# Narrower moving operands in the triangular inversions of a two-block hybrid layer

## The chip, the cores and the metric

The kernel is one program on one core of a Trainium2 chip. The metric is the device time of an execution in microseconds. Three executions of the kernel before are known, and one more was recorded by the hardware profiler. All times below are from these.

## What is computed

The reference runs two different transformer-like blocks, one after the other, on 256 tokens of width 2048, in float32. Only the two places that need the inverse of a triangular matrix matter here.

The first block holds a gated delta rule with 8 heads and chunks of 64 tokens:

```
lmat = where(strict, k_beta @ k.T * decay, 0)              # 64 x 64 per chunk and head
sol  = triangular_solve(eye + lmat, rhs, lower=True, unit_diagonal=True)
```

The second block holds a recurrence over tokens, forward and backward, with 16 heads of 64:

```
sa = S @ nkk_t
S  = S * w_t + sa b_t^T + v_t k_t^T
```

The kernel computes it in chunks of 64 tokens too, and each chunk needs the inverse of a unit triangular 64x64 matrix.

## The kernel before

Nearly all of the span is projections: weights come from memory in pieces, are split on ScalarE and VectorE into a high and a low part, and TensorE multiplies both by the activations (lines 267 to 290). The delta rule (about 570 to 790 us) is interwoven with the projection of a gated unit (`glu`, lines 608 to 610). The recurrence (about 2190 to 2720 us) runs alone: no projection lies beside it.

An inverse is built by doubling. Let T be the inverse of the block diagonal with blocks of size w. Level l (w = 2^l, l = 1 to 5) makes it into the one with blocks of 2w by two products with a mask between them:

1. the mask product, A times T, into one PSUM bank (`b[0]`);
2. VectorE multiplies it by the level's mask and keeps the w columns out of every 2w that the mask leaves, packed, in `i_p` (line 1151). At level 5 in the "tt" form it masks all 64 columns (line 1149);
3. the sum product, T times that, into a second place in PSUM (`b[1]`);
4. VectorE adds the result to the columns of T concerned (lines 1163 and 1160), and below level 5 transposes T into its second copy (line 1167).

So only 32 of a 64-column row are used by a level. `lower(ap, b)` is the strided view of them (runs of b out of 2b), `packed(ap, b)` the view of the first 32 columns as runs of b, `narrow(bank)` the four 64-column blocks of a bank.

In the **recurrence** one inversion works on 2 directions by 4 blocks by 2 halves of the partitions: 16 matmuls of 64x64 by 64 columns for each product (`blocks_pe`, line 1117). The two halves are products on opposite corners of the array, `half(0)` to `half(0)` and `half(1)` to `half(1)`. There are 16 inversions (8 pairs of heads, context and sequence), hence 160 products. The turns of `phases` (line 2005) weave the inversion (`V`) with the chunk steps (`C`), the preparation of the next unit (`P`) and the finishing of the last (`O`) on each engine, in the order of `PERIOD` (line 1565).

In the **delta rule** one inversion works on 4 blocks by 2 halves: 8 matmuls for each product (`halves_pe`, line 1063), 4 inversions, 40 products.

All these operands are float32, and the trace shows each float32 matmul as two records of TensorE, each with its own weight load (PEld): 5,120 records on line 1117 and 640 on line 1063.

In the kernel before every one of these matmuls moves 64 columns. The mask product moves all of T. The sum product moves the 32 packed columns of `i_p` twice, through a broadcast view. The last sum product of the "tt" form moves all 64 columns of `i_tt`.

Of the kernel before, what the change touches and what calls it, by code (L numbers as in the profile page):

```python
# [16 lines left out]
ALU = mybir.AluOpType  # L17
# [13 lines left out]
C = 64  # L31
# [62 lines left out]
def program(nc, d):  # L94

    ctx = ExitStack()
    with ctx:
        base = (nc.sbuf_base + 63) // 64 * 64

        def sb(name, shape, offset, dt=F32):  # L100
            return nc.alloc_sbuf_tensor_at(name, [P] + list(shape), dt, offset=base + int(offset * KB))
# [79 lines left out]
        i_a = sb("i_a", [4, C], TMP)  # L181
        i_t = sb("i_t", [4, C], TMP + 2)
        i_tt = sb("i_tt", [4, C], TMP + 4)
        i_p = sb("i_p", [4, C], TMP + 6)
# [245 lines left out]
        def settle(eng):  # L430


            eng.sem_inc(settled, 1)
# [619 lines left out]

        def halves_pe(pe, by_pe, out, lhs, rhs):

            for m in range(4):
                for r in (slice(0, C), slice(C, P)):
                    o, w = out[r, m * C:m * C + C], rhs[r, m, :]  # L1060
                    if w.shape[1] < C:
                        o, w = o.rearrange("p (a s) -> p a s", a=2), w.unsqueeze(1).broadcast_to([C, 2, C // 2])
                    mm = pe.matmul(o, lhs[r, m, :], w, start=True, stop=True)
            mm.then_inc(by_pe, 1)

        def invert_pe(pe, n, one):
            by_pe, by_dve, (i_a, i_t, i_tt, i_p), b, want = one
            for l in range(1, 6):
                pe.wait_ge(by_dve, n * 17 + (3 if l == 1 else 3 * l - 1))
                halves_pe(pe, by_pe, b[0], i_a, i_t)  # L1070
                yield
                pe.wait_ge(by_dve, n * 17 + 3 * l + 1)
                if l < 5:
                    halves_pe(pe, by_pe, b[1], i_tt, i_p[:, :, 0:C // 2])
                else:
                    halves_pe(pe, by_pe, b[1], i_p, i_tt)
                yield

        def invert_dve(dve, n, sets):
            inv_first_dve(dve, n, sets, d_mask)  # L1080
            yield
            for l in range(1, 6):
                inv_mask_dve(dve, n, sets, l, d_mask)
                yield
                inv_sum_dve(dve, n, sets, l)
                yield
# [3 lines left out]
        def lower(ap, b, first=0):  # L1090

            return ap.rearrange("p m (k s) -> p m k s", s=2 * b)[:, :, :, first:first + b]

        def packed(ap, b):

            return ap[:, :, 0:C // 2].rearrange("p m (k s) -> p m k s", s=b)

        def narrow(bank, first=0):
            return bank[:, first:first + 4 * C].rearrange("p (m s) -> p m s", m=4)

        def all4(mask):
            return k_masks[:, mask:mask + 1, :].broadcast_to([P, 4, C])

        def blocks_pe(pe, n, sets, k, outs, lhs, rhs):

            for swap in range(2):
                if not swap:
                    settle(pe)
                mm = [None, None]
                for m in range(4):  # L1110
                    for e in range(2):
                        r = half(e ^ swap)
                        w = rhs[e][r, m, :]
                        o = outs[e][r, m * C:m * C + C]
                        if w.shape[1] < C:
                            o, w = o.rearrange("p (a s) -> p a s", a=2), w.unsqueeze(1).broadcast_to([C, 2, C // 2])
                        mm[e] = pe.matmul(o, lhs[e][r, m, :], w, start=True, stop=True)  # L1117
            for e in range(2):
                mm[e].then_inc(sets[e][0], 1)

        def inv_mask_pe(pe, n, sets, l):
            for by_pe, by_dve, (i_a, i_t, i_tt, i_p), b, want in sets:
                pe.wait_ge(by_dve, n * 17 + (3 * l if l == 1 else 3 * l - 1))
            blocks_pe(pe, n, sets, 2 * l - 1, [s[3][0] for s in sets], [s[2][0] for s in sets], [s[2][1] for s in sets])

        def inv_sum_pe(pe, n, sets, l):
            for by_pe, by_dve, (i_a, i_t, i_tt, i_p), b, want in sets:
                pe.wait_ge(by_dve, n * 17 + (3 * l + 1))
            lhs = [i_p if l == 5 and want == "tt" else i_tt for _, _, (i_a, i_t, i_tt, i_p), b, want in sets]
            rhs = [i_tt if l == 5 and want == "tt" else i_p[:, :, 0:C // 2] for _, _, (i_a, i_t, i_tt, i_p), b, want in sets]  # L1130
            blocks_pe(pe, n, sets, 2 * l, [s[3][1] for s in sets], lhs, rhs)

        def inv_first_dve(dve, n, sets, all4):
# [9 lines left out]
        def inv_mask_dve(dve, n, sets, l, all4):  # L1143
            w = 2 ** l
            for by_pe, by_dve, (i_a, i_t, i_tt, i_p), b, want in sets:
                dve.wait_ge(by_pe, n * 10 + (2 * l - 1))
                m = all4(l)
                if l == 5 and want == "tt":
                    dve.tensor_tensor(i_p, narrow(b[0]), m, ALU.mult).then_inc(by_dve, 1)
                else:  # L1150
                    dve.tensor_tensor(packed(i_p, w), lower(narrow(b[0]), w), lower(m, w), ALU.mult)\  # L1151
                       .then_inc(by_dve, 1)

        def inv_sum_dve(dve, n, sets, l):
            w = 2 ** l
            for by_pe, by_dve, (i_a, i_t, i_tt, i_p), b, want in sets:
                dve.wait_ge(by_pe, n * 10 + 2 * l)
                if l == 5 and want == "tt":
                    out = lower(i_tt, w, w)
                    dve.tensor_tensor(out, lower(narrow(b[1]), w, w), out, ALU.add).then_inc(by_dve, 1)  # L1160
                else:
                    out = lower(i_t, w)
                    dve.tensor_tensor(out, packed(narrow(b[1]), w), out, ALU.add).then_inc(by_dve, 1)
            if l < 5:
                for by_pe, by_dve, (i_a, i_t, i_tt, i_p), b, want in sets:
                    dve.wait_ge(by_dve, n * 17 + (3 * l + 2))
                    dve.transpose(i_tt, i_t).then_inc(by_dve, 1)
# [127 lines left out]
        def dn_pe(pe, i):  # L1295
# [41 lines left out]
            pe.wait_ge(*dnv.at(i, "init"))  # L1337
            pe.wait_ge(*dna.at(i, "bv"))
            yield from invert_pe(pe, i, inv[0])
            pe.wait_ge(inv[0][1], i * 17 + 17)  # L1340
            for c in range(NCH):
# [632 lines left out]
        def half(a):  # L1974
            return slice(64 * a, 64 * a + 64)
# [306 lines left out]
        def inverse_pe(pe, j, x):  # L2282
            yield
            pe.wait_ge(j_done[1][1], inv_no(j, x) * 17 + 3)
            settle(pe)
            for l in range(1, 6):
                inv_mask_pe(pe, inv_no(j, x), jinv[x], l)
                yield
                inv_sum_pe(pe, inv_no(j, x), jinv[x], l)
                yield  # L2290
# [4 lines left out]
        def inverse_dve(dve, j, x):  # L2295
            dve.wait_ge(*pre_v[x].at(j, "im1"))
            inv_first_dve(dve, inv_no(j, x), jinv[x], all4)
            yield
            for l in range(1, 6):
                inv_mask_dve(dve, inv_no(j, x), jinv[x], l, all4)  # L2300
                yield
                inv_sum_dve(dve, inv_no(j, x), jinv[x], l)
                yield
# [1027 lines left out]
```

## Time and profile before

| What | Value |
|---|---|
| time of three executions, median (lowest to highest) | 3584.18 us (3581.43 to 3584.95) |
| the profiled execution's own time | 3591.9 us |
| its span, first to last instruction | 3590.1 us |
| mean granted clock of TensorE | 0.97 of full speed |
| PE busy, share of the span | 3381.0 us (94%), 28442 records |
| PEld (weight loads) | 2915.5 us (81%), 28442 records |
| DVE | 2470.7 us (69%) |
| ACT | 1588.0 us (44%) |

PE is TensorE's matmuls, PEld its weight loads, DVE is VectorE, ACT ScalarE. The busy time of PE counts every matmul from its start to its modelled end, and matmuls are pipelined, so 94% is not 94% of what the array can do: the pitch, the time from one start to the next, tells more than the length. A granted clock of 1.00 in a stretch is 2.4 GHz, 0.50 is 1.2 GHz.

### The profile page before, as it was taken

To read this page: it belongs to the slowest core of one execution; us is meant where nothing else is said; L and a number is where in the kernel's file an instruction comes from. 1 tells how busy PE (TensorE), PEld (TensorE's weight loads), DVE (VectorE), ACT (ScalarE), POOL (GpSimd) and SP (SyncE) were. 2 spreads that over 40 slices of the span, in tenths; PEclk is the share of its full clock that TensorE was granted. 3 is DMA by queue.
4 is the path that set the end of the run, shared out by engine and by line. 5 is a ranking of instruction groups with operands and counts; after the bars stand their busy time and mean duration, and the time that the engine had idled before them with its cause. 6 is when DMAs were issued, how large, how long until landed. Compare 5 with 4: busy or idle time off the path is not lost. (4 is left out here: it accounts for less than half of the span.)

```text
span 3590.1 us, 73988 instructions
## 1 busy us (share of the span) xinstructions
PE 3381.0 (94%) x28442; PEld 2915.5 (81%) x28442; DVE 2470.7 (69%) x4291; ACT 1588.0 (44%) x2475; POOL 248.0 (7%) x415
## 2 busy tenths in 40 slices
PE   9999998999899999999899987888888899999998
PEld 8998887788788888888788965766667788888887
DVE  5769995656777778777765864667665766666555
ACT  5547773334444444444212344444443444444433
POOL 0000000000000000111111202111110000000000
PEclk9999998999999999999999997999998999999999
DMA  5446662235455555776444720000003466665553
GB/s 196 180 154 241 247 251 82 83 118 189 162 184 184 183 186 186 260 244 246 157 170 172 275 69 12 7 7 7 8 6 129 165 225 226 225 224 202 190 188 134
DMA packets 94341, 572.25 MB, mean 159 GB/s; under 512 B 12657, under 2 KB 14961, under 8 KB 37521
## 3 DMA queue, kind: packets, MB, share of 16 engines
q1 hardware_dynamic: 72000, 493.49, 37.8%
q0 software_dynamic: 22096, 75.32, 6.1%
q8 instruction: 177, 2.90, 0.3%
q14 instruction: 68, 0.55, 0.0%
HBM read 566.66 MB, written 2.10 MB: 158 GB/s over the span
## 5 line engine op out<-in xcount | busy, mean ns | idle before, releaser
L246 ACT ACTIVATE w_hi<-raw 128x1024 fp32r<-128x1024 f32 (+1 forms) x877 | 908.8, 1041 | 948.9 <-PE po L290 638.4
L253 DVE TENSOR_TENSOR w_lo<-raw,w_hi 128x1024 fp32r<-128x1024 f32 x880 | 1044.5, 1199 | 176.5 <-ACT w_hi L246 166.1
L289 PE MATMUL po<-hh,w_hi 128*128 128x512 f32 x2816 | 991.1, 398 | 16.9 <-DVE hh L398 8.8
L290 PE MATMUL po<-hh,w_lo 128*128 128x256 f32 x2816 | 787.4, 280 | 0.0
L289 PEld LDWEIGHTS po<-hh,w_hi 128*128 128x128 f32 x2816 | 530.5, 188 | 146.8 <-issue 18.1
L290 PEld LDWEIGHTS po<-hh,w_lo 128*128 128x128 f32 x2816 | 532.3, 189 | 0.0
L289 PE MATMUL po<-ff,w_hi 128*128 128x512 f32 x1408 | 494.3, 397 | 3.2 <-DVE w_lo L253 3.2
L290 PE MATMUL po<-ff,w_lo 128*128 128x256 f32 x1408 | 393.0, 279 | 0.0
L289 PEld LDWEIGHTS po<-ff,w_hi 128*128 128x128 f32 x1408 | 264.9, 188 | 67.1 <-DVE w_lo L253 3.9
L267 PE MATMUL po<-hh,w_lo 128*128 128x256 f32 x928 | 266.3, 287 | 0.6 <-DVE w_lo L253 0.5
L290 PEld LDWEIGHTS po<-ff,w_lo 128*128 128x128 f32 x1408 | 265.8, 189 | 0.0
L268 PE MATMUL po<-hh,w_hi 128*128 128x256 f32 x928 | 262.5, 283 | 0.0
L269 PE MATMUL po<-hh,w_hi 128*128 128x256 f32 x928 | 262.5, 283 | 0.0
L1623 PE MATMUL po<-hh,w_hi 128*128 128x512 f32 x704 | 217.8, 391 | 0.0
L554 POOL DMA_DIRECT2D late_w<-ada_late x256 | 137.8, 539 | 1138.5 <-DVE late_sum L567 835.6
L492 DVE TENSOR_REDUCE f_sum<-po 128x512 f32 (+1 forms) x132 | 91.3, 692 | 141.8 <-PE po L290 141.8
L567 DVE SCALAR_TENSOR_TENSOR late_sum<-late_w,cve,late_sum 128x512 f32<-128x512 f32 x240 | 179.2, 747 | 9.0 <-DMA late_w<-ada_late 5.8
L267 PEld LDWEIGHTS po<-hh,w_lo 128*128 128x128 f32 x928 | 177.9, 192 | 6.0 <-issue 5.0
L268 PEld LDWEIGHTS po<-hh,w_hi 128*128 128x128 f32 x928 | 177.9, 192 | 0.2
L269 PEld LDWEIGHTS po<-hh,w_hi 128*128 128x128 f32 x928 | 177.9, 192 | 0.0
L608 PE MATMUL po<-hh,w_lo 128*128 128x256 f32 x512 | 155.1, 303 | 1.0 <-DVE pa L3042 1.0
L1623 PEld LDWEIGHTS po<-hh,w_hi 128*128 128x128 f32 x704 | 132.9, 189 | 27.7
(581 smaller groups left out, 6251.2 us busy)
## 6 DMA issues: line engine op xcount, KB each, us to landing
raw<-ffn_up SPq DMA_DIRECT2D x176, 1024.0 KB, 4.8
raw<-w_in SPq DMA_DIRECT2D x112, 1024.0 KB, 4.9
late_w<-ada_late POOLq DMA_DIRECT2D x256, 256.0 KB, 4.2
raw<-ffn_down SPq DMA_DIRECT2D x64, 1024.0 KB, 5.1
raw<-ada SPq DMA_DIRECT2D x32, 1024.0 KB, 7.0
raw<-w_out SPq DMA_DIRECT2D x32, 1024.0 KB, 4.8
raw<-ffn_down SPq DMA_DIRECT2D x32, 768.0 KB, 4.2
raw<-glu SPq DMA_DIRECT2D x16, 1024.0 KB, 4.8
```

The lines of the kernel that those rows point to most:

```text
L246: act.activation(w_hi[:, k % 4, 0:width], raw[:, k // 2 % ring, (k % 2) * PW:(k % 2) * PW + width], ACT.Copy).then_inc(hi_ready, 1)
L253: dve.tensor_tensor(w_lo[:, k % 4, 0:width], raw[:, k // 2 % ring, (k % 2) * PW:(k % 2) * PW + width], w_hi[:, k % 4, 0:width].bitcast(F32 ...
L267: pe.matmul(po[bank][:, 0:T], lo, act_hi[:, t, :], start=first and n == 0, stop=False)
L268: pe.matmul(po[bank][:, 0:T], hi, act_lo[:, t, :], start=False, stop=False)
L269: mm = pe.matmul(po[bank][:, 0:T], hi, act_hi[:, t, :], start=False, stop=end)
L289: pe.matmul(halves(bank), hi, pair[:, :, t, :], start=first and n == 0, stop=False)
L290: mm = pe.matmul(po[bank][:, 0:T], lo, pair[:, 0, t, :], start=False, stop=last and n == len(tiles) - 1)
L492: return dve.tensor_reduce(out, po[bank][:].rearrange("p (s t) -> p t s", s=2), AX.X, ALU.add)
L554: pool.dma_start(late_w[:, n % 4], d["ada_late"][n:n + 1].rearrange("a p w -> p (a w)")).then_inc(late_landed[n % 4], 16)
L567: dve.scalar_tensor_tensor(out, w, col, out, ALU.mult, ALU.add).then_inc(late_step, 1)
L608: pe.matmul(bank(i * per + o), lo, act_hi[:, t, :], start=first, stop=False)
L1623: mm = pe.matmul(po[o % 4][:].rearrange("p (s t) -> p s t", s=2), w, hh[:, :, part, t, :], start=half == 0 and n == 0 and w is lo, stop=ha ...
```

## The change

Every matmul of an inversion gets the 32 columns that its level uses, and no more. A new helper `moved` takes the moving operand as it is (3 dimensions: its width decides) or as a strided view (4 dimensions, runs of s), and gives the output 32 contiguous columns. The mask product below level 5 now moves `lower(i_t, 2 ** l)`; the "t" form does so at level 5 too. The sum product moves `i_p`'s 32 columns once. The last sum product of the "tt" form moves the upper 32 columns of `i_tt`. Only the mask product of level 5 in the "tt" form still moves 64 (128 of the recurrence's 2,560 matmuls, 32 of the delta rule's 320). VectorE reads the result from packed columns of PSUM where it read it strided, with the same number of elements.

```
+        def moved(out, r, m, rhs):
+            w = rhs[r, m]
+            if len(rhs.shape) == 3:
+                return out[r, m * C:m * C + rhs.shape[2]], w
+            k, s = rhs.shape[2:]
+            return out[r, m * C:m * C + k * s].rearrange("p (k s) -> p k s", s=s), w
...
         def halves_pe(pe, by_pe, out, lhs, rhs):
...
-                    o, w = out[r, m * C:m * C + C], rhs[r, m, :]
-                    if w.shape[1] < C:
-                        o, w = o.rearrange("p (a s) -> p a s", a=2), w.unsqueeze(1).broadcast_to([C, 2, C // 2])
+                    o, w = moved(out, r, m, rhs)
...
-                halves_pe(pe, by_pe, b[0], i_a, i_t)
+                halves_pe(pe, by_pe, b[0], i_a, lower(i_t, 2 ** l) if l < 5 else i_t)
...
-                    halves_pe(pe, by_pe, b[1], i_p, i_tt)
+                    halves_pe(pe, by_pe, b[1], i_p, i_tt[:, :, C // 2:C])
...
         def blocks_pe(pe, n, sets, k, outs, lhs, rhs):
...
-                        w = rhs[e][r, m, :]
-                        o = outs[e][r, m * C:m * C + C]
-                        if w.shape[1] < C:
-                            o, w = o.rearrange("p (a s) -> p a s", a=2), w.unsqueeze(1).broadcast_to([C, 2, C // 2])
+                        o, w = moved(outs[e], r, m, rhs[e])
...
         def inv_mask_pe(pe, n, sets, l):
...
+            rhs = [i_t if l == 5 and want == "tt" else lower(i_t, 2 ** l) for _, _, (i_a, i_t, i_tt, i_p), b, want in sets]
...
         def inv_mask_dve(dve, n, sets, l, all4):
...
-                    dve.tensor_tensor(packed(i_p, w), lower(narrow(b[0]), w), lower(m, w), ALU.mult)\
+                    dve.tensor_tensor(packed(i_p, w), packed(narrow(b[0]), w), lower(m, w), ALU.mult)\
...
         def inv_sum_dve(dve, n, sets, l):
...
-                    dve.tensor_tensor(out, lower(narrow(b[1]), w, w), out, ALU.add).then_inc(by_dve, 1)
+                    dve.tensor_tensor(out, packed(narrow(b[1]), w), out, ALU.add).then_inc(by_dve, 1)
```

No engine's instructions change their number or their order: on PE the inversion's matmuls stand where they stood, 32 columns wide in place of 64, and the queues of DVE, ACT, POOL and SP read the same.

## Rows read from the trace of the kernel before

**Rows 1.** The page's chain of work that ended last, shares of the span by line.

```profile
PE po L289 15%; PE po L290 8%; PE pa L1117 2%; PE po L1117 1%; DVE k_S L2407 0%; DVE k_ln L2463 0%; DVE k_ah L2235 0%; DVE j_p L1151 0%; PE pa L2335 0%; PE po L2352 0%; PE pa L2113 0%; PE pa L2352 0%; PE po L2087 0%; PE pa L2132 0%; PE pa L2049 0%
```

**Rows 2.** The recurrence: the chain's shares by line, then busy time in 50 us stretches.

```profile
by line: issue 14.3%; PE pa L1117 11.2%; PE po L1117 9.0%; DVE k_S L2407 2.6%; DVE k_ah L2235 2.2%; DVE j_p L1151 2.1%; PE pa L2113 2.0%; DVE k_ln L2463 2.0%; PE po L2087 1.9%; PE pa L2132 1.9%; PE pa L2049 1.8%; DVE k_nt L2261 1.7%; PE pa 
core 0: us, PE busy (x) PEld busy (x) DVE busy (x) ACT busy (x) POOL busy (x), PEclk, DMA share, GB/s
...
sum 500.00, PE 421.17 PEld 347.58 DVE 338.15 ACT 223.36 POOL 88.43; mean PE 42.12 PEld 34.76 DVE 33.82 ACT 22.34 POOL 8.84
```

**Rows 3.** Line 1117: its records, and who waited for it (us, times).

```profile
L1117 PEld LDWEIGHTS po<-j_p,j_work x1280: 129/135/227, 2204.7 to 2697.1; 64*64 64x64 f32 x183
L1117 PE MATMUL po<-j_p,j_work x1280: 218/218/366, 2204.7 to 2697.2; 64*64 64x64 f32 x183
...
  DVE j_p L1151: 58.7, 34
  DVE j_work L1163: 35.3, 37
  DVE j_p L1149: 6.4, 15
  DVE j_inv_c L1160: 4.5, 8
  DVE j_inv_l L1160: 4.4, 8
```

**Rows 4.** Line 1063: who waited for it (us, times).

```profile
  DVE i_t L1163: 19.4, 16
  DVE i_p L1151: 10.8, 10
```

**Rows 5.** Timeline of TensorE, one recurrence product from 2409 us (start us, length us).

```profile
2409.09 0.22 PE L1117 MATMUL pa<-j_inv_c,j_p 64*64 64x64 f32 x1
...
2409.85 0.22 PE L1117 MATMUL pa<-j_inv_c,j_p 64*64 64x64 f32 x1
```

**Rows 6.** Timeline of TensorE, line 2087: products on four quarters of the array.

```profile
2440.15 0.24 PE L2087 MATMUL pa<-k_ah,k_kh 64*64 64x64 f32 x1
...
2440.39 0.22 PE L2087 MATMUL po<-k_ah,k_kh 64*64 64x64 f32 x1
```

**Rows 7.** Timeline: 128-column weights with 2 (line 532) and 64 (line 1797) moving columns.

```profile
328.89 1.05 PE L532 MATMUL po<-ada_sel,ada_row 128*128 128x2 f32 x8
...
328.89 0.97 PEld L532 LDWEIGHTS po<-ada_sel,ada_row 128*128 128x128 f32 x8 [0.86 <-issue]
...
2111.81 2.54 PEld L1797 LDWEIGHTS po<-t_v,t_pt 128*128 128x128 f32 x22
```

**Rows 8.** Lines 532 (128 columns of weights) and 1680 (32, 256 moving): min/median/max ns.

```profile
L532 PEld LDWEIGHTS po<-ada_sel,ada_row x64: 186/192/192, 328.9 to 556.8; 128*128 128x128 f32 x64
...
L1680 PEld LDWEIGHTS pa<-n_sqs,n_sel x32: 106/110/110, 2005.1 to 2057.0; 128*32 128x32 f32 x32
L1680 PE MATMUL pa<-n_sqs,n_sel x32: 379/379/404, 2005.1 to 2057.3; 128*32 128x256 f32 x32
```

**Rows 9.** VectorE's steps of the inversion (min/median/max ns).

```profile
L1151 DVE TENSOR_TENSOR j_p<-pa,k_masks x64: 273/291/293, 2204.1 to 2692.0; 128x128 f32<-128x128 f32 x64
...
L1163 DVE TENSOR_TENSOR j_work<-pa,j_work x64: 279/292/293, 2206.7 to 2693.8; 128x128 f32<-128x128 f32 x64
```

**Rows 10.** Busy time and granted clock (PEclk) in chosen stretches, columns as in rows 2.

```profile
2253.80:2264.00 10.20, 9.63 (x134) 7.76 (x132) 4.47 (x13) 6.05 (x12) 1.41 (x2) 0.50 0.05 15
...
2315.00:2325.00 10.00, 7.86 (x171) 6.37 (x171) 5.45 (x18) 6.15 (x14) 1.02 (x2) 1.00 0.06 16
...
2414.30:2427.90 13.60, 12.53 (x108) 8.55 (x108) 3.97 (x15) 5.47 (x12) 1.41 (x2) 0.50 0.05 12
...
2690.00:2697.50 7.50, 5.90 (x170) 5.42 (x172) 5.31 (x19) 1.24 (x4) 0.00 (x0) 1.00 0.01 3
2697.50:2711.00 13.50, 12.05 (x125) 9.10 (x119) 4.11 (x14) 3.79 (x12) 0.00 (x0) 0.63 0.00 1
```

More of the change, by code:

```diff
@@ L1123, in inv_mask_pe @@
                 pe.wait_ge(by_dve, n * 17 + (3 * l if l == 1 else 3 * l - 1))
-            blocks_pe(pe, n, sets, 2 * l - 1, [s[3][0] for s in sets], [s[2][0] for s in sets], [s[2][1] for s in sets])
+            rhs = [i_t if l == 5 and want == "tt" else lower(i_t, 2 ** l) for _, _, (i_a, i_t, i_tt, i_p), b, want in sets]
+            blocks_pe(pe, n, sets, 2 * l - 1, [s[3][0] for s in sets], [s[2][0] for s in sets], rhs)
         def inv_sum_pe(pe, n, sets, l):
@@ L1129, in inv_sum_pe @@
             lhs = [i_p if l == 5 and want == "tt" else i_tt for _, _, (i_a, i_t, i_tt, i_p), b, want in sets]
-            rhs = [i_tt if l == 5 and want == "tt" else i_p[:, :, 0:C // 2] for _, _, (i_a, i_t, i_tt, i_p), b, want in sets]
+            rhs = [i_tt[:, :, C // 2:C] if l == 5 and want == "tt" else i_p[:, :, 0:C // 2] for _, _, (i_a, i_t, i_tt, i_p), b, want in sets]
             blocks_pe(pe, n, sets, 2 * l, [s[3][1] for s in sets], lhs, rhs)
```

## The prediction

> **What bounds the kernel now.** I read the page's chain first. The longest lines in it are projections, 289 and 290; line 1117, the recurrence's inversion, holds about 3% of the span [rows 1]. So the question belongs to one stage. In the recurrence, the chain by line and the table of stretches stand side by side: line 1117 holds 11.2% and 9.0% of 500 us, about 101 us, the largest share of any line, while VectorE is busy 338 of the 500 [rows 2]. No engine is full. The stage is a chain of handovers: a product on TensorE, a mask or a sum on VectorE, the next product. What counts there is how long a product takes from its first matmul to the end of its last. In the delta rule the products stand between those of the gated unit, which fill TensorE.
>
> **What a product costs, and what sets it.** One recurrence product is two streams, one per corner of the array, each of 16 records. The timeline of one stream has starts at 2409.09 and at 2409.85 with 13 steps between them: 0.76 / 13 = 58.5 ns a step [rows 5]. A step has two things in it that overlap: moving 64 columns and loading 64 columns of weights for the next.
> - *Moving.* 64 columns last 218 ns [rows 3], 256 last 379 [rows 8]: (379 - 218) / 192 = 0.84 ns a column, so 64 columns stream for 54 ns and 32 for 27.
> - *Loading.* 64 columns last 135 ns [rows 3], 32 last 110 [rows 8]: 0.8 ns a column, 51 ns for 64.
> - *Issue.* It isn't the limit: line 2087, whose products lie on four quarters of the array in place of two corners, starts 16 records from 2440.15 to 2440.39, 16 ns apart [rows 6], where line 1117 starts one every 29 ns.
>
> So moving and loading are nearly equal now, and the step of 58.5 ns is either's time with some 5 ns on top. The change halves the first and leaves the second. What a step does when only the load is long is read where weights of 128 columns meet few moving ones: the loads of 8 matmuls with **2** columns take 0.97 us from the first start to the last end, (0.97 - 0.19) / 7 = 111 ns a step, where 0.19 is the length of one such load [rows 8]; those of 22 matmuls with **64** columns take 2.54 us, (2.54 - 0.19) / 21 = 112 ns a step [rows 7]. Thirty-two times the columns, the same step: there the load sets it. Half such a load would be 56 ns.
>
> [...]
>
> **The change, part by part.**
> - *The steps of a product.* Bounds: unchanged at 58.5 ns, or 56, the half of 111. I take 58.5, the nearest row, which is this very load in this very place. The other end is 15 steps of 2.5 ns, 0.04 us a product; on the products that VectorE waited for (next point) 87 x 0.04 = 3.3 us.
> - *The end of a product.* The last matmul ends 27 ns sooner. This is worth something where VectorE stood waiting. In the recurrence it waited 34 + 37 + 8 + 8 = 87 times at lines 1151, 1163 and 1160 [rows 3]: 87 x 27 = 2.3 us. The 15 waits of line 1149 follow the product that keeps 64 columns. In the delta rule it waited 16 + 10 = 26 times [rows 4]: 0.7 us at most, since the gated unit's products stand behind. Together -3 us. Where VectorE was late anyway, its own queue (chunk steps, preparation) hides the gain.
> - *VectorE.* It reads packed columns of PSUM where it read strided ones. Line 1151 (strided) and line 1163 (packed) have the same size and take 291 and 292 ns [rows 9]: nothing, with no cover needed.
> - *The strided view.* At level 1 the moving operand is runs of 2 elements. No row shows such a read. It can't beat contiguous columns, so no gain; up to 54 ns for 32 columns it lies under the load and costs nothing beyond the 27 ns at the end. I take nothing. If runs of 2 took twice the old 54 ns, the 16 mask products of level 1 would grow by 15 steps of 50 ns each: +12 us.
> - *The clock.* I take no change; the other end is in the second rival.
>
> The sum is -3 us on the profiled execution of 3591.9 us (its span 3590.1). That execution stands 7.7 us above the median of 3584.18, and the difference carries over: **3581 us**. The terms' ends give 3577 to 3585. A measurement here can tell about 0.2%, 7.2 us, so my forecast is no change.
>
> **Rival 1, faster: the step falls.** If the 58.5 ns are moving time and a load of 64 rows and columns is cheaper than half of a full one, the step goes to 27 + 5 = 32 ns, 45% less. On 101 us of chain that is 46 us, and some 4 in the delta rule (40 products x 7 steps x 27 ns is 7.5, half of it hidden): 3534 us. VectorE's own work would be next to end late and may keep half: 3559. For it: none of these rows has 64-column weights with fewer than 64 moving columns. Against it: rows 7, and the load's 51 ns, which don't care what is moved. It decides if a step falls below 55 ns.
>
> **Rival 2, slower: TensorE is granted its low clock for longer.** The recurrence already runs partly at 1.2 GHz: 2253.8 to 2264 and 2414.3 to 2427.9 at 0.50 [rows 10], and three more such stretches of the recurrence, not shown, end as these two do while inversion products run. At the end of the recurrence the inversion's products held 1.00 (170 records in 7.5 us); then the chunk steps ran alone (125 in 13.5 us) and the clock fell to a mean of 0.63 [rows 10]. So these products are what keeps the clock up in the thin places, and the change takes half their columns away. At the low clock VectorE, as the measure of progress, is busy 8.4 of 23.8 us, at the full one 5.5 of 10 in a thin part of a turn [rows 10]: 10 us at the low clock cost 1 - 0.35 / 0.55, some 3.6 us; against its mean of 338 of 500 [rows 2], 4.8. Say 4.2. If each of the five stretches ends 5 us later (11 us) and two new ones of 10 us come (8 us), it is +19 - 3: 3600 us; half of the 19 gives 3591. I put its centre at 3596. Against it: thin stretches with 171 records in 10 us hold 1.00 [rows 10], the number of records stays, and so does the time of the loads; if those count as work, nothing changes. It decides once the low stretch that begins near 2414 us lasts clearly over 13.6 us.
>
> [...]
>
> **Rival 3, slower: the strided read** as priced above, 3593 us. That the change doesn't narrow the matmuls is no rival: the order of the changed program has them at 32 columns.
>
> **How the numbers follow.** Forecast 0.44, rival 1 0.15, rival 2 0.38, rival 3 0.03. Of the forecast 0.37 lies within 0.2% and 0.07 below, should the step also shrink to 56 ns. Rival 1 is faster throughout. Rival 2 in its milder forms (0.07) stays within, else it is slower (0.31). Faster 0.22, same 0.44, slower 0.34. Cases of both signs weigh much, so the forecast's own range, 3577 to 3585, stands beside the whole one, 3563 to 3606: it leaves out rival 1 nearly entire and the far end of rival 2, somewhat under 2 in 10.
>
> **What the changed profile would show.** Right: records of line 1117 about 191 ns long in place of 218, with starts in a stream still 56 to 59 ns apart; VectorE's waits on them shorter by about 0.03 us each; the recurrence within 5 us of its length; granted clocks as before. Wrong: steps near 32 ns (rival 1), or a recurrence longer by 10 us and more with more of it at 0.50 (rival 2), or steps of level 1's mask products longer than those of the other levels (rival 3).

## The result and the profile after

The changed kernel takes **3725.82 us** (median of 5 runs, 3720.63 to 3754.32), the kernel before, run beside it, 3584.95 us (5 runs, 3581.43 to 3599.81). The ratio is 1.0394, 95% interval 1.0368 to 1.0421: slower by about 141 us. The forecast was 3581 us, the range 3563 to 3606, and slower had a chance of 0.34.

The page of the changed kernel first: the busy times, TensorE's busy tenths and granted clock in 40 slices of the span, and the chain by engine and by line.

```profile
PE 3579.4 (95%) x28442; PEld 3093.9 (82%) x28442; DVE 2469.0 (66%) x4291; ACT 1589.7 (42%) x2475; POOL 243.7 (6%) x415
...
PE   9999998999899999998999879989998899999998
...
PEclk9999997989999999999999976565566999999999
...
PE 38%; DVE 2%; issue 1%; ACT 0%; DVEq 0%; POOL 0%; ACTq 0%
PE po L289 15%; PE po L290 7%; PE pa L1120 4%; PE po L1120 3%; PE pa L2326 1%; PE pa L2091 1%; PE po L2091 1%; PE pa L2352 1%; PE pa L2339 0%; PE pa L2053 0%; PE pa L2073 0%; PE po L2356 0%; PE pa L2356 0%; PE pa L2117 0%; PE po L2073 0%
```

And the line of the granted clock on the page of the kernel before:

```profile
PEclk9999998999999999999999997999998999999999
```

The number of matmuls is the same (28,442 before and after), nearly half of the inversion's columns are gone, and yet TensorE is busy 198 us longer, and VectorE as long as before (2469.0 against 2470.7 us). The inversion of the recurrence, line 1117 before, is line 1120 here. Its share of the page's chain went from 3% [rows 1] to 7%. The difference that meets the eye is the clock: eight slices in a row of 5 to 7 tenths where the kernel before has 9 almost throughout. They are the recurrence. The mean granted clock of the span went from 0.970 to 0.901. With the two levels 1.00 and 0.50 that is (1 - 0.970) / 0.5 x 3590.1 = 215 us at 1.2 GHz before and (1 - 0.901) / 0.5 x 3752.5 = 743 us after, 528 us more. (The profiled execution of the changed kernel is the slowest of the five; the other four had 0.906 to 0.908, which is 685 to 700 us.)

Two stretches of 50 us in the middle of the recurrence, by engine (busy us, records, then the granted clock, DMA share and GB/s), in the kernel before:

```profile
2300.00:2350.00 50.00, 43.09 (x1079) 36.59 (x1080) 36.80 (x112) 21.56 (x54) 10.15 (x14) 1.00 0.02 6
2350.00:2400.00 50.00, 41.03 (x952) 34.00 (x948) 36.54 (x112) 28.29 (x66) 11.76 (x16) 1.00 0.03 8
```

and in the changed kernel:

```profile
2300.00:2350.00 50.00, 47.88 (x722) 39.37 (x720) 24.96 (x81) 17.02 (x39) 7.32 (x11) 0.57 0.02 5
2350.00:2400.00 50.00, 47.86 (x848) 42.09 (x846) 29.76 (x91) 15.61 (x38) 5.61 (x8) 0.60 0.02 6
```

Read them across. By its records TensorE is *busier* after (47.88 us of 50 against 43.09), and so are its weight loads (39.37 against 36.59); but it gets through 722 records in place of 1079, and VectorE, whose work per turn has not changed, through 81 instructions in place of 112. The clock is 0.57 where it was 1.00. The longer busy time is in part its effect: records last longer at the low clock, as the lines of line 1120 below show. Timed from the last turn of the attention to the last matmul with `k_bd` (line 2423 before, 2427 after) the recurrence takes 683.7 us, before 553.0: 131 us of the 162 by which the two spans differ. Most of the rest lies in the delta rule. The whole recurrence as one stretch, before and after:

```profile
2171.60:2724.60 553.00, 455.83 (x9843) 371.80 (x9842) 349.23 (x1072) 239.69 (x571) 96.11 (x131) 0.90 0.03 8
```

```profile
2196.30:2880.00 683.70, 623.30 (x9843) 521.49 (x9842) 348.02 (x1072) 241.09 (x571) 92.05 (x131) 0.59 0.02 6
```

The work is the same, 9843 records of TensorE and 1072 instructions of VectorE. By the clocks, (1 - 0.90) / 0.5 x 553.0 = 111 us of it ran at the low level before and (1 - 0.59) / 0.5 x 683.7 = 561 us after. TensorE, idle for 97 us of this stage before, is idle for 60 us now.

The step itself did what the forecast said at the full clock. One stream of a product at the full clock in the changed kernel, by the timeline (start us, length us), to be held against [rows 5]:

```profile
2369.62 0.21 PE L1120 MATMUL pa<-j_work,j_a_c 64*64 64x32 f32 x1 [0.82 <-DVE j_inv_c L1145]
2369.67 0.22 PE L1120 MATMUL pa<-j_work,j_a_c 64*64 64x32 f32 x1
...
2370.52 0.22 PE L1120 MATMUL pa<-j_work,j_a_c 64*64 64x32 f32 x1
```

15 steps in 0.90 us, 60 ns, with 32 columns; [rows 5] had 58.5 ns with 64. Another product, where the low clock is granted:

```profile
2288.00 0.31 PE L1120 MATMUL pa<-j_work,j_a_c 64*64 64x32 f32 x1
2288.12 0.29 PE L1120 MATMUL pa<-j_work,j_a_c 64*64 64x32 f32 x1
...
2289.62 0.29 PE L1120 MATMUL pa<-j_work,j_a_c 64*64 64x32 f32 x1
```

15 steps in 1.62 us, 108 ns. Over all neighbouring records of a stream the median step is 58 ns at the full clock and 107 ns at the low one, in both kernels. What changed is how many fall on each: counted from the starts in the trace, 338 of line 1117's 4,800 steps run at the low clock before (7%); after, 3,540 of the 4,560 steps with 32 columns (78%).

Records of line 1120 (min/median/max ns) and VectorE's waits on it (us, times), against those in [rows 3]:

```profile
L1120 PEld LDWEIGHTS po<-j_p,j_work x1280: 129/223/228, 2229.5 to 2851.4; 64*64 64x64 f32 x183
L1120 PE MATMUL po<-j_p,j_work x1280: 192/291/313, 2229.5 to 2851.5; 64*64 64x32 f32 x183
...
L1120 PE MATMUL pa<-j_inv_c,j_p x128: 219/219/313, 2253.5 to 2817.4; 64*64 64x32 f32 x128
...
  DVE j_p L1155: 99.5, 54
  DVE j_work L1167: 68.2, 62
```

The first two lines are mostly of the low clock, with medians of 223 ns for a load and 291 ns for a matmul; the third, of level 5, is mostly of the full clock, at 219 ns. VectorE waits 54 times for 1.84 us each where it waited 34 times for 1.73 us, and 62 times for 1.10 us where it waited 37 times for 0.95 us: more often, and longer.

### The profile page after: what moved, and what is told of

Its sections match the earlier page's. It is cut to its first block and busy times, and to the rows that moved or that the text cites. A ratio compares the mean times of both kernels' runs of the same rounds, so it can differ in the third digit from the quotient of the medians.

```text
span 3752.5 us, 73988 instructions
## 1 busy us (share of the span) xinstructions
PE 3579.4 (95%) x28442; PEld 3093.9 (82%) x28442; DVE 2469.0 (66%) x4291; ACT 1589.7 (42%) x2475; POOL 243.7 (6%) x415
```

## Experiments

The theory after the result: the change lowers the number of columns that TensorE moves in the thin places of the recurrence, the low clock is granted for longer, and everything on TensorE there runs slower. The rivals: the strided read, VectorE's packed reads of PSUM, or the narrow matmul as such. All runs are put beside runs of the kernel before on the same chip; their median is 3586.75 us for the first four kernels, 3585.85 us for the half dose, the other columns and the first two fills, and 3592.96 us for the last three runs (twice the columns, the last two fills). The time at the low clock is worked out from span and mean clock, as above.

### Moving the 32 columns twice

The changed kernel with everything that it reads and packs, but each 32-column view goes through the array twice, as in the kernel before:

```diff
-                return out[r, m * C:m * C + rhs.shape[2]], w
+                return o.rearrange("p (a s) -> p a s", a=2), w.unsqueeze(1).broadcast_to([C, 2, C // 2])
             k, s = rhs.shape[2:]
-            return out[r, m * C:m * C + k * s].rearrange("p (k s) -> p k s", s=s), w
+            return o.rearrange("p (a k s) -> p a k s", a=2, s=s), w.unsqueeze(1).broadcast_to([C, 2, k, s])
```

> The changed kernel, but every 32-column view is moved twice into neighbouring columns of PSUM (through a broadcast), so that each matmul streams 64 columns again; the strided view, the packed reads of VectorE and the order stay. Theory (the clock is granted less because the inversion's matmuls stream half the columns): back to the kernel before, 3575 to 3605 us, low clock (0.50) for about 200 to 260 us of the span in place of 744. Rival A (the strided view or the packed reads are what costs): stays near 3726 us, 3700 or more.

Measured: 3589.78 us (10 runs) against 3586.75, ratio 1.0009 (0.9989 to 1.0029). The loss is gone. The stretch of the recurrence that stood at 0.57 above, in this kernel:

```profile
2300.00:2350.00 50.00, 43.48 (x958) 35.56 (x954) 33.80 (x104) 26.04 (x60) 11.05 (x16) 0.97 0.03 8
```

The span's mean clock is 0.971, some 208 us at the low level, as before the change. The strided view and VectorE's packed reads are both still in it, so neither is the cause. What is left is the number of columns that a matmul moves and writes; moving and writing were not told apart.

### The same columns without a stride

The mask product moves the first 32 columns, which lie side by side, in place of those of the level, so that it computes another matrix.

```diff
-                halves_pe(pe, by_pe, b[0], i_a, lower(i_t, 2 ** l) if l < 5 else i_t)
+                halves_pe(pe, by_pe, b[0], i_a, i_t[:, :, 0:C // 2] if l < 5 else i_t)
...
-            rhs = [i_t if l == 5 and want == "tt" else lower(i_t, 2 ** l) for _, _, (i_a, i_t, i_tt, i_p), b, want in sets]
+            rhs = [i_t if l == 5 and want == "tt" else i_t[:, :, 0:C // 2] for _, _, (i_a, i_t, i_tt, i_p), b, want in sets]
```

> The changed kernel, but the mask product below level 5 moves the first 32 contiguous columns of T in place of the strided 32 (so it computes another matrix). Theory (clock): as the changed kernel, 3705 to 3755 us, since 32 columns are streamed as before. Rival A (the strided read costs): most of the 141 us is gone, under 3640 us.

Measured: 3727.5 us (2 runs), ratio 1.0394 (1.0342 to 1.0445), the ratio of the change itself. The stride costs nothing that shows, from the other side too.

### Each stage alone

The change in the delta rule alone, and in the recurrence alone. In each the other stage has its former products and VectorE reads them as before.

```diff
-            rhs = [i_t if l == 5 and want == "tt" else lower(i_t, 2 ** l) for _, _, (i_a, i_t, i_tt, i_p), b, want in sets]
+            rhs = [i_t for _, _, (i_a, i_t, i_tt, i_p), b, want in sets]
...
-            rhs = [i_tt[:, :, C // 2:C] if l == 5 and want == "tt" else i_p[:, :, 0:C // 2] for _, _, (i_a, i_t, i_tt, i_p), b, want in sets]
+            rhs = [i_tt if l == 5 and want == "tt" else i_p[:, :, 0:C // 2] for _, _, (i_a, i_t, i_tt, i_p), b, want in sets]
```

(This is the delta rule alone; for the recurrence alone the same is done in `invert_pe`.)

> Only the delta rule's inversion moves 32 columns; the recurrence moves 64 as before. Theory (clock): the delta rule's stage ends later by what its low-clock stretches add (its low clock grew from about 34 to 103 us between 556 and 782 us of the profiled executions, the stage's end moved by some 22 us): 3595 to 3615 us. Rival (all of the loss lies in the recurrence, which runs alone): 3580 to 3592 us.

> Only the recurrence's inversion moves 32 columns; the delta rule moves 64 as before. Theory (clock): the larger part of the loss, 3695 to 3715 us, low clock in the recurrence (2190 to 2860 us) as in the changed kernel. Rival (the two stages share the loss evenly): near 3655 us.

Measured: the delta rule alone 3613.52 us (7 runs), ratio 1.0050 (1.0019 to 1.0081), some 280 us at the low clock. The recurrence alone 3718.1 us (4 runs), ratio 1.0362 (1.0315 to 1.0409), some 660 us. The two losses, 0.50% and 3.62%, add up to 4.1%, within the interval of the whole. The first time is within what was expected and the second 3 us above it. Each stage pays by itself. The delta rule loses too, although the gated unit's products stand beside its inversion: the cover that the prediction named there did not hide this.

### Half of the dose

Only the mask product moves 32 columns; the sum product moves its 32 twice again.

```diff
-                return out[r, m * C:m * C + rhs.shape[2]], w
+                o = out[r, m * C:m * C + C]
+                if rhs.shape[2] == C:
+                    return o, w
+                return o.rearrange("p (a s) -> p a s", a=2), w.unsqueeze(1).broadcast_to([C, 2, C // 2])
```

> The changed kernel, but the sum product of both inversions moves its 32 columns twice again, as before; only the mask product moves 32. Theory (the clock falls because fewer columns stream through TensorE): half of the products are narrow, so the loss lies between nothing and the change's 141 us, and the low-clock time of the span between 219 and 744 us; I expect 3620 to 3690 us. Rival (the narrow product itself is slow, its read or its write, whatever the clock): the loss is in proportion, 3655 us, at an unchanged granted clock of 0.97.

Measured: 3630.99 us (4 runs), ratio 1.0137 (1.0111 to 1.0162), mean clock 0.950, some 363 us at the low level. In the recurrence:

```profile
2300.00:2350.00 50.00, 43.28 (x997) 36.94 (x994) 36.59 (x114) 24.27 (x58) 11.47 (x16) 0.90 0.03 9
2350.00:2400.00 50.00, 44.57 (x828) 35.50 (x825) 29.44 (x91) 23.28 (x55) 6.51 (x10) 0.77 0.03 8
```

The time is in the expected range, and the clock is not the unchanged 0.97 of the rival. A little under half of the narrow products (1,280 of 2,720 matmuls, since the mask products of level 5 in the "tt" form were not narrowed) bring about a third of the loss (1.37%, 49 of 141 us) and 28% of the added low-clock time (148 of 528 us). The loss is nearer to the time at the low clock than to the number of narrow products; in proportion to the products the ratio would have been 1.0185, outside the interval.

### Other columns beside the narrow products

The changed kernel, and ahead of each of the recurrence's products two matmuls more whose result nobody reads. They move as many columns as the change took away; the 16 matmuls that count stay 32 wide.

```diff
                 if not swap:
                     settle(pe)
+                    for e in range(2):
+                        pe.matmul(outs[e][half(e), 4 * C:8 * C], lhs[e][half(e), 0, :], sets[e][2][1][half(e)],
+                                  start=True, stop=True)
```

> The changed kernel, and in each product of the recurrence's inversion two more matmuls ahead of it, that move 256 columns each with 64x64 weights into half of the bank that nothing reads: more work, and as many moved columns per product as before the change, although the 16 matmuls that count stay 32 wide. Theory (moved columns keep the clock up): low clock in the recurrence falls back to about that of before, and the time falls although work was added, to 3610 to 3670 us (the two matmuls take some 0.25 to 0.5 us in each of 160 products, of which a part is hidden). Rival (the narrow matmuls themselves cost, or lower the clock, whatever runs beside them): the added work comes on top, 3765 to 3800 us.

Measured: 3724.71 us (4 runs), ratio 1.0377 (1.0342 to 1.0412): neither figure. But the clock answered. The mean is 0.937, some 470 us at the low level in place of 743, and two stretches and the whole recurrence read:

```profile
2300.00:2350.00 50.00, 44.02 (x1024) 36.27 (x1020) 33.30 (x102) 19.07 (x49) 5.85 (x8) 0.99 0.02 5
2350.00:2400.00 50.00, 46.43 (x903) 37.41 (x904) 27.85 (x87) 24.64 (x56) 11.46 (x16) 0.91 0.03 8
...
2190.20:2853.90 663.70, 594.90 (x10482) 481.55 (x10482) 342.63 (x1072) 240.74 (x571) 93.00 (x131) 0.77 0.02 7
```

In the recurrence that is (1 - 0.77) / 0.5 x 663.7 = 305 us at the low level, in place of 561; it is not back at the 111 us of before, as I had expected. In the first of these stretches the narrow matmuls ran at 0.99, with other columns sent through the array ahead of them. So the rival in its second form, that the narrow matmul lowers the clock whatever runs beside it, is out.

The time stayed the same as that of the change. An estimate of why: the fill isn't cheap. Its step is 266 ns at the full clock by the starts in the trace, and each stream has two of its records in a product, so 160 x 2 x 266 ns = 85 us, and more where the clock is low; my expectation had 40 to 80 us, of which I had taken a part to be hidden. Against it stand 273 us less at the low clock. The change paid 162 us of span for its 528 us, 0.31 us for each, so they are worth 85 us. The two cancel, and 1 us less was measured; no run separates them.

### Twice the columns

The kernel before, with each matmul of the recurrence's products moving its columns twice, 128 in place of 64.

```diff
-                        w = rhs[e][r, m, :]
-                        o = outs[e][r, m * C:m * C + C]
-                        if w.shape[1] < C:
-                            o, w = o.rearrange("p (a s) -> p a s", a=2), w.unsqueeze(1).broadcast_to([C, 2, C // 2])
+                        o, w = wide(outs[e], r, m, rhs[e][r, m, :])
```

(`wide` gives a view of both halves of the bank and the moving operand through a broadcast of 2.)

> The kernel before, but each matmul of the recurrence's inversion products moves its columns twice, 128 in place of 64, the second copy into the half of the bank that nothing reads. Theory (the step is the longer of the weight load, 58 ns, and of the time to stream the columns): 128 columns hold the step at 100 to 110 ns at the full clock, 8 steps of some 49 ns more in each of 160 products are 63 us, of which TensorE pays nearly all: 3620 to 3660 us at a granted clock of 0.97 or above. Rival (the load alone holds the step even at 128 columns): no slower than before, and up to 15 us faster by a higher clock.

Measured: 3674.5 us (2 runs), ratio 1.0232 (1.0186 to 1.0277). The timeline of one stream:

```profile
2381.50 0.27 PE L1121 MATMUL pa<-j_work,j_a_l 64*64 64x128 f32 x1
2381.61 0.27 PE L1121 MATMUL pa<-j_work,j_a_l 64*64 64x128 f32 x1
2381.71 0.27 PE L1121 MATMUL pa<-j_work,j_a_l 64*64 64x128 f32 x1
```

The median step at the full clock is 109 ns, 0.85 ns a column: here the columns set it. Over the three widths, 58 ns for 32, 58 for 64 and 109 for 128, the step fits the longer of a load's time and the columns' time. The step is the theory's, and the time lies above its range (3620 to 3660 us). The size was wrong by a miscount: a stream has 16 records in a product, as the prediction says, not 8. 160 x 15 x 51 ns are 122 us, of which 83 showed. The clock in this recurrence:

```profile
2300.00:2350.00 50.00, 47.27 (x920) 41.85 (x916) 31.75 (x101) 20.50 (x50) 9.84 (x14) 1.00 0.02 6
2350.00:2400.00 50.00, 44.73 (x820) 38.18 (x817) 29.46 (x91) 22.86 (x54) 6.08 (x9) 1.00 0.03 8
```

This row beside that of the change is the shortest sign that busy time by records doesn't tell the clock: 47.27 us busy at 1.00, 47.88 us busy at 0.57 (there lengthened by the low clock itself).

### Filling the idle places of the kernel before

If columns hold the clock up, the kernel before may gain by columns where TensorE stands idle before its low stretches. `fill_pe` issues matmuls of 128x128 weights (the identity) and 256 columns into a bank's half that nobody reads.

```diff
             for e in range(2):
+                if first_unit(j, x):
+                    fill_pe(pe, 3 if e else 12)
                 pe.wait_ge(*pre_g[x].at(j, f"kh{e}"))
...
             pe.wait_ge(*ota.at(7, "q"))
+            fill_pe(pe, 8)
             pe.wait_ge(low_a, 3)
```

> The kernel before, and 23 matmuls of 128x128 weights and 256 columns in the three waits of TensorE that open the recurrence (4.9, 6.6 and 2.1 us idle between 2171 and 2191 us of the span), their result unread. Theory (a stretch of idle TensorE starts the 37.5 us of low clock at 2171.9): those 37.5 us shrink to under 15, and as TensorE is busy in about 60% of them the kernel gains 3 to 12 us, 3573 to 3582 against 3585. Rival (the low stretch comes from the small matmuls that follow, or the filler is late and holds up the work): no change or 2 to 6 us slower.

The second kernel adds, in `phases`, a fill at the end of the loop's turn:

```diff
                 tile(i * 2 + 2, 0)
+                if eng is nc.tensor:
+                    eng.wait_ge(j_done[0][1], inv_no(i * 2 + 3, "c") * 17 + 17)
+                    fill_pe(eng, 5)
```

> As the filler at the start, and 5 such matmuls more at the end of each turn of the recurrence's loop, where TensorE waits 3.4 us at 2411.6 before 13.7 us of low clock (and again near 2544). Theory: these two stretches go too, 3 to 12 us less than the filler at the start alone, 3564 to 3580. Rival: the 2.2 us of filler come late in each of three turns and hold up the chunk that follows, 3 to 7 us slower than the filler at the start alone.

Measured: at the start alone 3588.33 us, ratio 1.0004 (0.9986 to 1.0023); with the turns 3589.18 us, ratio 1.0010 (0.9993 to 1.0028), 12 runs each (one of the second kernel took 7627 us and is not in its ratio). The gains of 3 to 12 us that the theory had for each did not come. At the start the low clock did go: the 50 us that begin 11.6 us before the end of the attention had a clock of 0.62 in the kernel before, and 0.90 with the fill. The rows, of the kernel before:

```profile
2160.00:2210.00 50.00, 30.55 (x313) 24.31 (x315) 12.61 (x36) 24.79 (x56) 9.45 (x14) 0.62 0.06 20
```

and of the kernel with the fill at start and turns:

```profile
2147.10:2197.10 50.00, 38.69 (x423) 32.02 (x424) 14.41 (x42) 25.71 (x57) 11.89 (x18) 0.90 0.07 20
```

In its profile the recurrence took 541.1 us in place of 553.0, so it ran once more, with a third kernel that also fills the gaps of the last chunk:

```diff
                     mm.then_inc(Q.did(f"u{e}_{s}"), 1)
+                if x == "l" and isinstance(j, int) and j == 7:
+                    fill_pe(pe, 1)
...
                     mm.then_inc(Q.did(f"d{e}_{s}"), 1)
+                if x == "l" and isinstance(j, int) and j == 7:
+                    fill_pe(pe, 3)
```

> The kernel before with filler at the start and at the loop's turns, once more. In the profile its recurrence took 541.1 us against 553.0 before, but the runs showed no gain. Theory (the gain of the stage is real and variation of the other stages hid it): 8 to 14 us under the kernel before. Rival (the stage gains in the profiled execution alone): within 5 us of the kernel before.

> As the filler at the start and the turns, and filler also between the steps of the last chunk, where the trace of before has 34.1 us of low clock from 2701.0 with TensorE mostly idle. Theory (its small matmuls lie on the chain, and run at half speed there): low clock in the span falls from 160 to about 130 us and the recurrence gains 2 to 6 us more in the profile. Rival (the filler holds up the chain's matmuls): the recurrence is 2 to 8 us longer than without the filler in the last chunk.

Measured: once more 3586.47 us, ratio 0.9981 (0.9962 to 0.9999), the recurrence 549.7 us in this profile (and 13.7 us at 0.50 from 2407.7 us on, near the place where the kernel before has its own from 2414.3); with the last chunk 3589.23 us, ratio 0.9990 (0.9970 to 1.0010), the recurrence 552.6 us. The expectation for the last chunk failed: its profile has the same 180 us at the low level as the one without it, not 130, and its recurrence is 2.9 us longer, which its rival had. No version here is shown to beat the kernel before by more than the scatter of these runs. The gain of 8 to 14 us expected of the repeated kernel is not borne out, and a small gain of a few us is neither shown nor excluded: the two ratios of the same kernel average 0.9996. Some 36 to 51 us less at the low clock in their profiles (mean clocks 0.975 and 0.977) bought next to nothing, while the change paid 0.31 us for each such us. Those stretches lie where TensorE waits most (30.55 us busy of 50 in the row above), so a faster clock there finds little to shorten, and the fill takes its own time; which of the two weighs more was not separated.

## Why the prediction was wrong

**The step that failed is "The clock. I take no change"**, and with it the price of rival 2. The mechanism was named there: the change takes half of the columns of the products that keep the clock up, and TensorE is granted its low clock for longer. Its size was off by a factor of ten: five stretches of the recurrence 5 us longer and two new ones of 10 us, 45 us in all, against 450 us measured there (561 - 111), and the delta rule, which the rival left out, lost 0.50% alone. Its price per us, 0.42, was too high but of the right order: the recurrence grew by 131 us, 131 / 450 = 0.29.

The sign by which it was to be told held at once: "the low stretch that begins near 2414 us lasts clearly over 13.6 us". In the changed kernel the table of stretches has there, and just before (by time, not by work: its recurrence begins 25 us later):

```profile
2372.50:2416.90 44.40, 43.38 (x608) 36.03 (x604) 20.94 (x64) 11.77 (x30) 5.52 (x8) 0.50 0.01 2
...
2420.30:2444.20 23.90, 23.01 (x383) 19.95 (x382) 15.91 (x48) 9.92 (x23) 4.19 (x6) 0.50 0.01 3
```

Why was it priced so low? Two readings led there.

- *The rows of the high clock were read as a reserve.* [rows 10] shows 171 records in 10 us at 1.00, and the text set that against the rival: the number of records stays, and so does the time of the loads. But a record's time was 58 ns of load *and* 54 ns of columns then; the change leaves the first and halves the second. The runs show which of the two counts here: the changed kernel and the one that moves its columns twice have the same matmuls and the same loads, and the stretch from 2300 us had 0.57 in the one and 0.97 in the other. The busy time of the loads can't tell it, 39.37 us of 50 against 35.56 us, because a load lasts longer at the low clock.
- *Only the thin places were priced.* The rival lengthened five known low stretches. What it should have asked is what the busy middle of the recurrence, 2300 to 2400 us at 1.00, would do with half the columns. The answer is the 0.57 and 0.60 above.

The Trainium skill, "TensorE: Matmul & The Clock Gate", section "What's actually happening", has the throttled state as the default that activity releases, and the trace agrees: with fewer columns the recurrence falls back to it, with a mean of 0.59 in place of 0.90. The Trainium skill, same page, section "Why this matters for your kernels", puts a fall in the middle of a kernel down to idle gaps between bursts of matmuls. By that rule the low stretch from 2372.5 us would not have come: the longest idle time of TensorE in the 15 us ahead of it is 0.90 us, shorter than the gaps which that section names, and in the stretch itself TensorE is busy 43.38 of 44.40 us and the clock stays at 0.50. Here the measurement decides: the same matmuls and loads had the low clock with 32 columns and the high one with 64.

Point by point, the rest of the working:

- *The step stays at 58.5 ns*: right. 58 ns at the full clock with 32 columns. The Trainium skill, same page, section "Back-to-back issue gap", says that in a stream of loads and matmuls both set the spacing. The trace agrees: 58 ns for 32 and for 64 columns, as [rows 7] had it for a longer load, and 109 ns for 128, where the columns take over.
- *The last matmul ends 27 ns sooner*: wrong, and the whole of the forecast's -3 us rested on it. At the full clock a record with 32 columns lasts 219 ns (the level 5 line of line 1120 above; 1,053 of 1,086 such records last 219 ns or more) where one with 64 lasted 218 [rows 3]; 21 alone reach 192 ns. The last record of a stream with 32 columns has 219 ns each time that it ran at the full clock. At the low clock it is 291 ns against 311, but lost there in the longer steps. VectorE's waits grew in place of shrinking.
- *VectorE's packed reads and the strided view cost nothing*: right. Line 1155, which was 1151 [rows 9], has 274/292/293 ns, and the two runs that kept or removed the stride differ from their partners by less than their intervals.
- *Rival 1, the step falls to 32 ns*: out, by the same 58 ns.
- *Where the 131 us of the recurrence come from*: the chain by line over the recurrence, before and after (the lines are cut off at their end in the view):

```profile
by line: issue 13.0%; PE pa L1117 10.1%; PE po L1117 8.1%; DVE k_S L2407 2.3%; DVE k_ah L2235 2.0%; DVE j_p L1151 1.9%; PE pa L2335 1.9%; PE po L2352 1.8%; PE pa L2113 1.8%; DVE k_ln L2463 1.8%; PE pa L2352 1.8%; PE po L2087 1.7%; PE pa L21
```

```profile
by line: PE pa L1120 19.6%; PE po L1120 17.0%; issue 4.4%; PE pa L2326 3.9%; PE pa L2091 3.3%; PE po L2091 3.2%; PE pa L2352 2.8%; PE pa L2339 2.6%; PE pa L2053 2.6%; PE pa L2073 2.5%; PE po L2356 2.4%; PE pa L2356 2.4%; PE pa L2117 2.4%; P
```

The inversion's line goes from 18.2% of 553.0 us, 101 us, to 36.6% of 683.7 us, 250 us, and VectorE's lines are no longer among the first. A product's 15 steps are 49 ns longer at the low clock, 0.74 us, so 160 products at 78% in place of 7% are 84 us longer in sum; the line's part of the chain grew by more, because more of its products lie on the chain. The prediction read the stage as a chain of handovers between two engines that are not full. At the low clock, by this chain, TensorE sets the pace nearly alone.

## What to carry to other kernels

When each matmul brings its own weights, look which is longer, the load or the moved columns. Here, with 64 columns of weights, the step was 58 ns for 32 and for 64 moved columns and 109 ns for 128: cutting from 64 to 32 saved nothing on TensorE's step, and it cost the clock, which came back when the columns did. Before narrowing an operand ask what the stage's clock rests on, and price the whole stage at 0.50 and not the thin places alone. A busy share of TensorE by records did not tell it here; the granted clock of the stretch does, beside the number of records that get done in it.

## What was not expected

TensorE at 47.88 us busy of 50, with loads in flight for 39.37 us, was granted 0.57, and the kernel with twice the columns got 1.00 at 47.27 us busy. A little under half of the narrow products brought 28% of the low-clock time that all of them brought. And removing some 36 to 51 us of the low clock of the kernel before, in places where TensorE mostly waits, did not make it measurably faster.
